# The last block of a two-block decoder: the first 128 tokens run ahead of the second from the last norm to the first expert gather

## What is computed

```python
x  = x + g1 * y                                   # y = mixed @ w_out, the out projection
h2 = rms_norm(x, norm2_g) * (1.0 + sc2) + sh2
q  = (xb @ wq).reshape(128, 8, 2, 128)            # 8 heads, two half queries each
s  = einsum('tphq,phkq->tphk', q, keys)           # 128 sub-keys per half
top_s, top_i = top_k(s, 16)
cand = top_s[:, :, 0, :, None] + top_s[:, :, 1, None, :]      # 16 x 16 sums
best_s, best_c = top_k(cand.reshape(128, 8, 256), 16)
idx = i1 * 128 + i2                               # 16384 experts
g   = softmax(best_s)
act = gelu(einsum('tpkd,td->tpk', u_tab[idx], xb))
out = einsum('tpk,tpkd->td', g * act, v_tab[idx])
```

## Time and profile before

| | |
|---|---|
| median of 3 runs | 2059.43 us (2057.61 to 2061.79) |
| the profiled execution | 2058.97 us |
| its span in the trace | 2057.0 us |
| TensorE, VectorE, ScalarE, GpSimd busy | 90%, 67%, 41%, 15% of the span |
| bytes by GpSimd's queue | 268.45 MB in 256 gathers |

### The profile page before, as it was taken

How to read it: one execution, slowest core, us unless ns; L and a number is a source line. 1 busy time by engine, 2 the same in 40 slices (tenths; PEclk the granted TensorE clock), 3 DMA queues, 4 the chain that set the end, 5 groups by cost and what they waited for, 6 DMA issues and landing times. The chain is left out here.

```text
span 2057.0 us, 27112 instructions
## 1 busy us (share of the span) xinstructions
PE 1851.0 (90%) x10504; PEld 1442.4 (70%) x10504; DVE 1383.0 (67%) x2669; ACT 843.3 (41%) x1588; POOL 306.9 (15%) x354
## 2 busy tenths in 40 slices
PE   7999998999999999899999999898997776877776
PEld 6999897899999998879898799684543222332222
DVE  5697566677667755767776577778576576675654
ACT  5333556633353344565234444433332333332323
POOL 0000212000000002300000000004443333343331
PEclk9999999999999999999999999999999999999999
DMA  7675541567556754327664133049999999999996
GB/s 265 203 233 179 171 150 62 185 205 250 179 194 223 240 190 137 125 83 235 201 227 154 62 104 110 21 144 400 420 421 421 421 421 421 421 421 421 422 421 267
DMA packets 223638, 505.54 MB, mean 246 GB/s; under 512 B 8244, under 2 KB 174870, under 8 KB 190742
## 3 DMA queue, kind: packets, MB, share of 16 engines
q1 hardware_dynamic: 186438, 235.29, 34.9%
q0 software_dynamic: 36864, 268.45, 31.4%
q10 hardware_dynamic: 208, 0.06, 0.0%
HBM read 502.72 MB, written 1.05 MB: 245 GB/s over the span
## 5 line engine op out<-in xcount | busy, mean ns | idle before, releaser
L278 DVE TENSOR_TENSOR LOWS<-RAW,HIGH 128x2048 fp32r<-128x2048 f32 (+2 forms) x150 | 343.3, 2298 | 31.0 <-ACT HIGH L266 30.4
L266 ACT ACTIVATE HIGH<-RAW 128x2048 fp32r<-128x2048 f32 (+2 forms) x150 | 287.7, 1926 | 126.3 <-DMA RAW<-in_ffn_w_down 34.7
L287 PE MATMUL PB<-HTR,HIGH 128*128 128x256 f32 (+2 forms) x1088 | 313.9, 289 | 0.0
L288 PE MATMUL PB<-HTR,HIGH 128*128 128x256 f32 (+2 forms) x1088 | 311.6, 286 | 0.0
L289 PE MATMUL PB<-HTR,LOWS 128*128 128x256 f32 (+2 forms) x1088 | 311.2, 286 | 0.0
L2475 PE MATMUL PB<-HIF,HTF 128*128 128x512 f32 x420 | 200.8, 611 | 55.6 <-ACT HTF L2708 55.6
L2475 PE MATMUL PB<-RAW,HTF 128*128 128x512 f32 x356 | 177.1, 631 | 53.4 <-ACT HTF L2708 53.4
L287 PEld LDWEIGHTS PB<-HTR,HIGH 128*128 128x128 f32 (+1 forms) x1088 | 204.4, 188 | 5.8 <-issue 0.2
L288 PEld LDWEIGHTS PB<-HTR,HIGH 128*128 128x128 f32 (+1 forms) x1088 | 202.7, 186 | 5.5
L289 PEld LDWEIGHTS PB<-HTR,LOWS 128*128 128x128 f32 (+1 forms) x1088 | 202.7, 186 | 4.2
L2475 PEld LDWEIGHTS PB<-HIF,HTF 128*128 128x128 f32 x420 | 77.4, 192 | 169.6 <-ACT HTF L2708 89.0
(11 more groups left out here) (412 smaller groups left out, 4039.9 us busy)
## 6 DMA issues: line engine op xcount, KB each, us to landing
RAW<-in_ffn_w_gate SPq DMA_DIRECT2D x32, 1024.0 KB, 5.5
RAW<-in_ffn_w_up SPq DMA_DIRECT2D x32, 1024.0 KB, 5.7
RAW<-in_ffn_w_down SPq DMA_DIRECT2D x32, 1024.0 KB, 5.1
RAW<-in_w_in SPq DMA_DIRECT2D x23, 1120.0 KB, 5.8
RAW<-in_w_mod SPq DMA_DIRECT2D x20, 1024.0 KB, 5.2
BIG<-in_ffn_w_gate SPq DMA_DIRECT2D x12, 1024.0 KB, 6.5
BIG<-in_ffn_w_up SPq DMA_DIRECT2D x12, 1024.0 KB, 8.0
BIG<-in_ffn_w_down SPq DMA_DIRECT2D x12, 1024.0 KB, 5.0
```

The source lines that it names most:

```text
L266: e.activation(u.h, u.raw, ACT.Copy).then_inc(*high_done.up())
L278: e.tensor_tensor(u.l, u.raw, u.h.bitcast(F32), ALU.subtract).then_inc(*low_done.up())
L287: e.matmul(o, lh, rh, start=k == 0, stop=False)
L288: e.matmul(o, lh, rl, start=False, stop=False)
```

## The change

Only the stretch from the out projection to the first sixty gathers is rewritten.

- Query tiles are not split any more; four of them (0 to 3) go to `RAW` slots, and the other four (`LATE`) straight into the slots of `HIF` that the out projection's high parts leave free. SyncE issues the keys first, then one tile of each kind after each tile of the out projection.
- Block 0 goes alone through the norm, the transposes and the shift. VectorE's part of its norm (`first_norm_vector`) stands ahead of the last gate and add of the out projection, and the first four keys are turned ahead of product 6. The product for heads 0 and 1 is made for each block apart (`UNITS`), block 0's first. The normed and shifted tokens are written once, in float32, without the split halves.
- Head 0 of block 0 is selected in two parts: the best 8 of each 128 scores, the 64 sums of them, the best 8 of those and their indices; these eight gathers may start (`index_done` counts them apart). Then come the other eight. Head 1's selection ("alone" pieces) is moved into the loop, between the dot products of gathers 0 to 5, and the pieces of the next pairs are moved later.
- The 13 places become free in another order: five at once, two after block 1's product for heads 0 and 1, two after the halves at gathers 3 and 8, and four after those at 20, 32, 44 and 56.

```diff
-            got["wq"] = [plan(wq[:, :, j * 256:(j + 1) * 256], (8, 256), query_done.at(j + 1), 1, split=j < WHOLE,
+            got["wq"] = [plan(wq[:, :, j * 256:(j + 1) * 256], (8, 256), query_done.at(j + 3), 1, split=False,
                               slots=NS - 1)
-                         for j in range(8)]
+                         for j in range(4)]
...
+            for j in range(4):
+                lows(e, SECOND["out"][j])
+                for b in range(2):
+                    if (j, b) == (3, 1):
+                        first_norm_vector(e)
...
+                if n == 6:
+                    keys_tensor(e, 0, 4)
+                mm3(e, PB[n % 4][:, 0:256], turned_halves(s), weight_halves(w, slice(0, 256))).then_inc(*out_done.up())
...
-        QUERY_AT = {3 + 7 * x: (4 + x // 2, x % 2) for x in range(8)}
+        UNITS = [(0, 0), (1, 0), (0, 1), (1, 1)] + [(j, None) for j in range(2, 8)]
+        QUERY_AT = {1: (4, 0), 3: (4, 1), 5: (5, 0), 8: (5, 1)}
+        QUERY_AT.update({14 + 6 * x: (6 + x // 2, x % 2) for x in range(8)})
...
-        PIECES = [("norm", 0, 0, 0)]
+        PIECES = [("norm", 0, 0, 0)] + [("alone", 1, n, n // 4) for n in range(0, 23, 4)]
+        PIECES += [("gates", 0, 1, 6), ("norm", 0, 1, 8)]
         for p in range(1, 8):
-            at = 32 * p - 30
+            at = 11 if p == 1 else 32 * p - 24
...
+            w = weights_of(0)
+            e.wait_ge(x_done.sem, X_MIX + 6)
+            for k in range(8):
+                e.wait_ge(*(h2_s if k % 4 > 1 else h2_v).next())
+                for c in range(2):
+                    x = e.matmul(PB[c][:, 0:128], w[:, k, c * 128:(c + 1) * 128], HT_WHOLE[:, k, 0, :], start=k == 0, stop=k == 7)
+            x.then_inc(*query_done.up())
+            e.wait_ge(x_done.sem, X_MIX + 8)
+            keys_tensor(e, 1, 2)
+            keys_tensor(e, 2, 3)
+            scores(0)
+            query(1, 0)
+            query(1, 1)
+            keys_tensor(e, 3, 5)
+            scores(1)
+            e.wait_ge(keys_read.sem, 3)
+            turned_back(0)
...
+        def first_norm_vector(e):
+            rstd_of_block(e, 0, 3)
+            e.wait_ge(*rs_done.next())
+            for i in (1, 3):
+                e.tensor_scalar(HN[0][:, i, :], X[:, 0, i * 256:(i + 1) * 256], RSTD[:, 0:1], None,
+                                ALU.mult).then_inc(*hn_v.up())
...
+            sums = WK[:, 1, 0:64]
+            in_turn(e.tensor_tensor(sums.rearrange("p (a b) -> p a b", a=8), ts[0][:, lo].unsqueeze(2).broadcast_to([128, 8, 8]),
+                                    ts[1][:, lo].unsqueeze(1).broadcast_to([128, 8, 8]), ALU.add))
+            in_turn(e.max(BS[:, 0, 0, lo], sums))
+            in_turn(e.max_index(BI[:, 0, lo].bitcast(U32), BS[:, 0, 0, lo], sums))
+            decoded(0, 8, 8, 3, 7)
...
-                if g in (0, 16):
-                    e.wait_ge(index_done.sem, g // 16 + 1)
+                if g in (0, 8, 16):
+                    e.wait_ge(index_done.sem, g // 8 + 1)
...
-            load(len(TILES))
-            e.wait_ge(query_done.sem, 8)
+            wq = A["peer_wq_2"][0].rearrange("(k p) n -> p k n", p=128)
+            for x in range(4):
+                load(SECOND["wq"][x].n + 1)
+                e.dma_start(LATE[x], wq[:, :, (4 + x) * 256:(5 + x) * 256]).then_inc(*late_in[x].up())
+            e.wait_ge(query_done.sem, 10)
```

More of the change, by code:

```diff
@@ L210, in build @@
         FILLED2 = (3, 6, 13, 15, 19, 23, 25, 27, 29, 37, 41, 43, 45, 47)
-        WHOLE = 2
         def plan_second():
@@ L1047, in dot_place @@
             return PB[(2, 3, 4, 7)[h % 4]][:, (h // 4) * 256:(h // 4) * 256 + 128 * (b + 1)]
[L1049 to L1081, removed]
         def hybrid_vector(e, l):
@@ L2277, in mix_turn_vector @@
             turn_count["v"] += s
+        X_MIX = X_AFTER["mix"] - 8
         def mix_out_vector(e):
@@ L2315, in mix_out_scalar @@
             mix_turn_scalar(e, 1)
-            project_out_scalar(e, SECOND["out"])
+            for j in range(4):
+                highs(e, SECOND["out"][j])
         def mix_out_tensor(e):
@@ new lines, in peer_vector @@
+            lo, hi = slice(0, 8), slice(8, 16)
+            src = [SC[:, 0, 0, x, :] for x in range(2)]
+            ts, ti = ([m[:, x, 0, :] for x in range(2)] for m in (TS, TI.bitcast(U32)))
+            work = [WK[:, 0, x * 128:(x + 1) * 128] for x in range(2)]
+            e.wait_ge(score_read.sem, 1)
+            e.wait_ge(count_in.sem, 16)
+            e.max(ts[0][:, lo], src[0])
+            in_turn(e.max(ts[1][:, lo], src[1]))
+            e.max_index(ti[0][:, lo], ts[0][:, lo], src[0])
@@ new lines, in peer_scalar @@
+            sqrt_ready(e)
+            squares_of(0, 0, 768, 5)
+            keys_copy(0, 4)
+            squares_of(1, 0, 768, 6)
+            squares_of(0, 768, 1024, 7)
+            sqrt_scalar(e, RSTD[:, 0:1])
+            e.wait_ge(*rs_done.last())
+            for i in (0, 2):
+                e.activation(HN[0][:, i, :], X[:, 0, i * 256:(i + 1) * 256], ACT.Copy,
+                             scale=RSTD[:, 0:1]).then_inc(*hn_s.up())
+            for i in (1, 3):
+                e.wait_ge(turned.sem, TURNED + i + 1)
+                for x in range(2):
+                    shifted(0, 2 * i + x, 4 + i, x)
@@ new lines, in peer_scalar @@
+            squares_of(1, 768, 1024, 8)
+            query_copy(0)
+            keys_copy(1, 2)
+            score(0)
+            keys_copy(2, 3)
+            query_copy(1)
+            keys_copy(3, 5)
+            score(1)
+            sqrt_scalar(e, RSTD[:, 1:2])
+            e.wait_ge(*rs_done.last())
+            for i in range(4):
+                e.activation(HN[1][:, i, :], X[:, 1, i * 256:(i + 1) * 256], ACT.Copy,
+                             scale=RSTD[:, 1:2]).then_inc(*hn_s.up())
+            for kc in range(8):
+                e.wait_ge(turned.sem, TURNED + 5 + kc // 4)
+                shifted(1, kc, 4 + 3 * (kc // 4), kc % 4)
@@ L2693, in peer_scalar @@
+            query_copy(2)
+            softs = {at: (p, which) for kind, p, which, at in PIECES if kind == "gates"}
             for batch in BATCHES:
```

363 lines of the change are left out of this document (224 added, 139 removed).

## The result

2041.46 us, median of 4 runs (2039.74 to 2043.84), against 2058.64 (4 runs): ratio 0.9914, 95% interval 0.9902 to 0.9927. Forecast were 2040.0 and a range of 2033 to 2050. The profiled execution took 2043.84 us, span 2042.0.

The account below looks back on a forecast made before the run. The gather loop was taken as bound by bytes, 2.49 us a gather. 2057.0 - 23.4 + 2.8 + 1.6 = 2038.0 us of span, plus 1.97 and 0.46, gave 2040.4, say 2040; range 2033 to 2050.

Parts of the forecast that it names:

- What bounds the kernel, and where the end comes from: Gather loop: bound by bytes, 2.49 us a gather; the end is set by gather 8's landing plus later starving, tail 11.9.
- When gather 0 is issued: From the out projection's last products to the first gather's issue: block 0 alone and a shorter selection, 18.1 us earlier.
- The two query tiles: At gather 8's landing: query tiles 6 and 7, formerly beside the first gathers, are in before; 5.3 us earlier.
- 2.8 us of starving at gather 13, and 1.6 of clock: Gather 13 waits for gather 5's mixing, 2.8 us late; one 3.2 us stretch of TensorE at half speed loses 1.6 us.
- Gathers 8, 10 and 16 come out within a microsecond of their time, none adds to it: Early gather loop: these three gathers were to add nothing to the 2.8 us of starving at gather 13.
- From 14 on TensorE keeps up, hardly: Gathers from 14 on: six need 14.2 us of TensorE against 15.0 of DMA, so no loss was counted.
- as summed: Case that the whole run comes out as the terms add up: 2036.5 to 2045 us, chance 0.58.
- TensorE becomes the bound of the opening: Rival, first gathers: more half clock, or VectorE's dot products holding the mixings back; 2045 to 2052 us, chance 0.22.
- The query tiles were not all in by 1370: Sign, ahead of the gather loop: all query tiles were to have landed before 1370 us in the new profile.
- a dip wider than one gather: Sign against the prediction: a DMA share dip, expected between 1400 and 1415 at 3 to 5 us, wider than one gather.
- the last dot product: Sign at the end of the gather loop: VectorE's last dot product at about 2026 us, then the same tail of 11.9.

Follow-up runs that it names:

- Light halves: The changed kernel with one of eight matmuls in every query half inside the loop, queries of heads 2 to 7 left incomplete: 2035.23 us, ratio 0.9886.

## Why the prediction came out right

- **What bounds the kernel, and where the end comes from.** Right. 421 GB/s and a share of 1.01 again, 2.49 us a gather while nothing else is in the way, 559.1 us against 559.3 behind gather 34, tail 11.9.
- **When gather 0 is issued: 18.1 us earlier.** 18.0 (A 35.12 to 17.12), and the steps stand one by one. Counted from the gate's start (in brackets what the sum had): norm at 5.39 (5.33), query 0's product at 7.50 (7.38) for 3.81 (3.65), first MAX at 13.09 (12.93), the first part of the selection 3.74 (3.8), issue at 17.12 (17.03). Where rows exist for each piece and the order is written down, adding them up works. How much the other place of block 0's norm would cost I had not asked; it is 3.3 on this path.
- **The two query tiles: 5.3 us at gather 8.** As to the first landing, it took 6.0 us, below the 6.6 I took and inside the bounds of 5.5 and 7.9. The Trainium skill ("DMA: Bandwidth & Descriptors", "Anatomy of one DMA") would have had 4.4 us by the estimate in the prediction; the row lies 1.6 above it. But the tiles' absence was not worth a term of its own in the changed kernel: with 2 MB put back beside the first gathers B did not grow, since what the transfers gained, waiting for places took.
- **2.8 us of starving at gather 13, and 1.6 of clock.** Nearly right at gather 13, by a way that was not the forecast one. 4.4 us were counted there; the lateness at gather 13 is 5.9, or 4.6 without the first gap's 1.3, and its issue came 37.3 us after the first where the sum, with the clock, has 36.8. But 3.2 of it was there at gathers 8 and 9 already. "Gathers 8, 10 and 16 come out within a microsecond of their time, none adds to it" was wrong: by the sum's own terms gather 1's mixing ends at 1390.2, so gather 8 lands at 1397.1 where fed it would land at 1397.0. It had no slack at all, and the half clock, counted only for gather 13, stood ahead of gather 8 as well. Block 1's `h2` was ready at 1376.7 (I had put about 1375; 0.9 us is left of that once the 0.8 by which the gate itself started later is taken off), its product took 9.04 us at the half clock, and gather 8 was issued at 1393.85, on the end of gather 1's mixing.
- **"From 14 on TensorE keeps up, hardly".** The mis-sized term: put at nothing, it was 3.1 us between gathers 14 and 28, 2.0 of them at gather 21. From 1440 on it is right: 98.70 us busy of 99, clock 1.00, DMA share 1.01. The average did keep up; what the sum had no term for is the reserve, and that is the likely reason. Before, gathers 13 to 24 landed 12 to 16 us after their issue, so five or six were out at a time; now they landed 6.5 to 10 us after it, so about three were out, and two issues with a query half between them are 5.2 us apart. Light halves leave 0.3 of the 3.1. At gather 11 VectorE also waits 7.37 us for a score that TensorE reaches behind its mixings, with gathers that have landed standing behind the wait, and I had priced the engines' work and not this order; but with the wait at 4.60 and TensorE's hole gone gather 22 landed no earlier, so how much of the 3.1 is its doing stays open.
- **The first gap.** Gather 1 landed 3.8 us after gather 0 although it was issued 1.45 after it; before had company there (2.6 us between the two), and no row showed it. Its cause is open. Where the queue had run short it came again: gather 9 was issued 1.3 us after gather 8 and landed 4.3 after it.

The books: 3.3 us more starving and 1.3 for the first gap, less 0.6 for the quicker first landing and less 0.7 that the kernel before itself lost behind gather 8 (624.65 us for 247 gathers, against 630.2 with 6.3 of lateness in them now). That is 3.3; the forecast 19.0 less 3.3 is 15.7, and 15.4 to 15.8 were found. The median, 2041.46 against 2040, lies nearer to the forecast than the mechanism does, and that is luck: 1.4 to 1.8 us of its gain lie outside of A and B. Of the rivals, "as summed" stands in the time, and "TensorE becomes the bound of the opening" is the mechanism that was at work, with 3.3 us more starving where I had priced 5 or more. The query tiles were not all in by 1370 (DMA ran at 348 GB/s for them until about 1372), and no engine waited for one. By a sign that the prediction named itself, a dip wider than one gather, its account of the starving was wrong: 7.7 us are three gathers, and the last dot product came at 2030.1 and not at about 2026.

## What to carry to other kernels

When a stage is bound by transfers, moving its start earlier is worth the full time only as long as the engines that free the buffers can follow: write down for each buffer which instruction frees it, and add up the list of that engine up to each release, not only its share. An average that keeps up is not enough when few transfers are out: ask how long the longest lump on that list is, and whether the transfers that are out last as long. An engine that works in order and waits for a late result holds back arrived work that stands behind the wait, so place such a piece where its input is surely there, even if it comes two turns later. Then look at the landings and not only at the wait that went. Before moving a short step off or onto a path, look at what hole it leaves on TensorE, because the clock that follows can cost as much as the step itself.

## What the runs showed of the hardware

- TensorE's clock came back at half (0.50, 1.2 GHz) after 2 us with 0.20 or 0.36 us of work in them, and the product that followed took 5.44 instead of 3.81, or 9.04 instead of 7.34. Three float32 matmuls of no use, 2.6 us of work in all, kept it at 1.00 (2.4 GHz). That activity lifts the clock and sparse work lets it go is what the Trainium skill says too ("TensorE: Matmul & The Clock Gate", Part 1).
- The first 1 MB gather, with the last query tile still arriving for about 0.7 us of its time, landed 6.0 us after its issue (5.7 to 6.3 in the other runs of that opening), the next one 3.8 us after it (3.0 to 4.8). While enough gathers were out, each landed 2.4 to 2.5 us after the one before; where they ran short, up to 4.3.
- The 1 MB query tiles ran at 348 GB/s with a DMA share of 1.10, the gathers at 421 with 1.01: the share alone does not tell how many bytes pass.
